# The load of x in column quarters at the head of a two-model transformer kernel

## The reference

```python
h = rms_norm(x, norm_pre[l])        # x * rsqrt(mean(x*x)) * gain
proj = h @ w_in[l]                  # [512, 2048] @ [2048, 5952], then split in 12 parts
... three kinds of attention on the parts, gates, w_out ...
x = x + rms_norm(y, norm_post[l])
```

## Time and profile before

| | |
|---|---|
| median of 3 runs | 3525.47 us (3524.55 to 3526.89) |
| the profiled execution's own time | 3524.82 us |
| its span | 3523.1 us |
| PE busy | 3397.5 us, 96% |
| VectorE busy | 1795.1 us, 51% |
| ScalarE busy | 1099.3 us, 31% |
| DMA over the span | 122 GB/s mean, 429.95 MB |
| mean granted TensorE clock | 0.986 |

### The profile page before, as it was taken

How to read it: one execution, slowest core, us unless ns; L and a number is a source line. 1 busy time by engine, 2 the same in 40 slices (tenths; PEclk the granted TensorE clock), 3 DMA queues, 4 the chain that set the end, 5 groups by cost and what they waited for, 6 DMA issues and landing times. The chain is left out here.

```text
span 3523.1 us, 50023 instructions
## 1 busy us (share of the span) xinstructions
PE 3397.5 (96%) x17285; PEld 2742.2 (78%) x17285; DVE 1795.1 (51%) x3258; ACT 1099.3 (31%) x1768; POOL 152.2 (4%) x218
## 2 busy tenths in 40 slices
PE   7999999999999999999997999999997999999997
PEld 6878878678788788786885888878786888878786
DVE  5564675445565557754456332625734332635643
ACT  3232242242241422522323222523323322423331
POOL 1101001000111010010010000000000000000000
PEclk9999999999999999999998999999998999999999
DMA  7636415215675363160454333133333333123242
GB/s 270 199 118 198 125 37 175 68 69 193 184 243 183 115 188 95 32 205 7 138 180 151 97 95 89 31 99 99 117 124 110 90 95 95 49 87 99 79 155 95
DMA packets 183848, 429.95 MB, mean 122 GB/s; under 512 B 18166, under 2 KB 25777, under 8 KB 177240
## 3 DMA queue, kind: packets, MB, share of 16 engines
q1 hardware_dynamic: 151144, 297.65, 26.3%
q0 software_dynamic: 28992, 104.43, 9.7%
q10 hardware_dynamic: 3504, 25.22, 1.8%
HBM read 406.15 MB, written 24.75 MB: 122 GB/s over the span
## 5 line engine op out<-in xcount | busy, mean ns | idle before, releaser
L681 PE MATMUL bank<-wlo,act_hi 128*128 128x512 f32 (+1 forms) x3968 | 1554.7, 392 | 8.8 <-DVE zone L1597 6.1
L683 PE MATMUL bank<-whi,act_lo 128*128 128x512 f32 (+1 forms) x3968 | 1537.9, 388 | 0.0
L682 PE MATMUL bank<-whi,act_hi 128*128 128x512 f32 (+1 forms) x3968 | 1536.8, 387 | 0.0
L1548 DVE TENSOR_TENSOR wlo<-stage,whi 128x1024 fp32r<-128x1024 f32 (+1 forms) x496 | 598.2, 1210 | 753.8 <-ACT whi L1184 751.5
L1184 ACT ACTIVATE whi<-stage 128x1024 fp32r<-128x1024 f32 (+1 forms) x496 | 514.9, 1048 | 1479.9 <-PE bank L683 734.8
L681 PEld LDWEIGHTS bank<-wlo,act_hi 128*128 128x128 f32 x3968 | 746.7, 188 | 178.2 <-issue 17.8
L683 PEld LDWEIGHTS bank<-whi,act_lo 128*128 128x128 f32 x3968 | 746.3, 188 | 153.3
L682 PEld LDWEIGHTS bank<-whi,act_hi 128*128 128x128 f32 x3968 | 747.1, 188 | 146.8 <-issue 1.0
L1563 DVE SCALAR_TENSOR_TENSOR macc<-wmod,csil,macc 128x512 f32<-128x512 f32 x360 | 269.9, 750 | 106.7 <-DMA wmod<-in_w_mod 76.9
L2415 POOL DMA_DIRECT2D wmod<-in_w_mod x192 | 136.9, 713 | 1706.2 <-DVE macc L1563 1675.0
L744 PE MATMUL bank<-zone 128*128 128x128 f32 x1024 | 134.6, 275 | 0.0
(11 more groups left out here) (239 smaller groups left out, 2269.7 us busy)
## 6 DMA issues: line engine op xcount, KB each, us to landing
stage<-in_w_in SPq DMA_DIRECT2D x352, 512.0 KB, 3.8
wmod<-in_w_mod POOLq DMA_DIRECT2D x192, 512.0 KB, 4.5
stage<-in_w_out SPq DMA_DIRECT2D x128, 512.0 KB, 4.1
out<-Y ACTq DMA_DIRECT2D x20, 1024.0 KB, 5.6
zone<-out SPq DMA_DIRECT2D x4, 4096.0 KB, 14.3
stage<-in_w_in SPq DMA_DIRECT2D x16, 320.0 KB, 3.7
Y<-in_x ACTq DMA_DIRECT2D x4, 1024.0 KB, 9.3
rpb_tiles<-rpb_pad POOLq DMA_DIRECT2D x16, 224.0 KB, 7.6
```

What stands on the lines that cost most here:

```text
L681: pe.matmul(out, hi_x, lo_w, start=(k == 0), stop=False)
L682: pe.matmul(out, hi_x, hi_w, start=False, stop=False)
L683: mm = pe.matmul(out, lo_x, hi_w, start=False, stop=(k == KC - 1))
L1548: dve.tensor_tensor(wlo[:, j % RH, :, 0:width], stage[:, j % RS, :, 0:width], whi[:, j % RH, :, 0:width].bitcast(F32), ALU.subtract).then_ ...
```

## The change

x is loaded in four column quarters (512 features of all 512 tokens, runs of 2 KB) in place of four token tiles (runs of 8 KB), and these loads stand first in ScalarE's queue. PE waits for quarter k // 4 ahead of the turn of tile k, in place of all four parts ahead of the panel. The stores of x go from behind tile 3 to behind tile 15 in ScalarE's order, in both layers. The waits for x and for the residual's second half move to the sums of squares. GpSimd issues panel 0's eight loads of `w_mod` ahead of the bias tiles, in layer 0 only.

```diff
@@ turns (PE)
+                if blk == 0 and n0 == 0 and k % 4 == 0:
+                    pe.wait_ge(boot_x[k // 4], 16)
@@ head of the layer (PE)
-                for t in range(TT):
-                    pe.wait_ge(boot_x[t], 16)
@@ turned_then_saved (ScalarE)
-                    if k == 2 * LEAD - 1:
+                    if k == KC - 1:
                         for t in range(TT):
-                            act.wait_ge(boot_x[t], 16)
                             act.wait_ge(prep.sem, prep.at(0, l, t + 1 - TT))
                             act.dma_start(x_dram[:, t, :], Y[:, t, :]).then_inc(x_saved.sem, 16)
@@ squares_between (ScalarE)
+                    if t == 0:
+                        for q in range(DM // PW):
+                            act.wait_ge(boot_x[q], 16)
                     if 0 <= t < TT:
+                        act.wait_ge(prep.sem, prep.at(0, l, t + 1 - TT))
@@ start of the queue (ScalarE)
+            for q in range(DM // PW):
+                act.dma_start(Y[:, :, q * PW:(q + 1) * PW], x_in[:, :, q * PW:(q + 1) * PW]).then_inc(boot_x[q], 16)
             act.sem_inc(exp_done.sem, exp_done.credit)
...
             act.activation(ctmp[:, :], JOB[0][:, 0:KC], ACT.Tanh, scale=0.5).then_inc(boot_act, 1)
-            for t in range(TT):
-                act.dma_start(Y[:, t, :], x_in[:, t, :]).then_inc(boot_x[t], 16)
@@ GpSimd
+                if l == 0:
+                    mod_loads(l, 0)
                 bias_tiles(l)
-                with pool.Fori(0, NIN) as p:
+                with pool.Fori(1 - l, NIN) as p:
                     mod_loads(l, p)
```

## The result

The change makes the kernel slower: 3532.99 us median (3529.72 to 3536.71, 19 runs) against 3524.75 us (3520.81 to 3527.53, 19 runs) of the kernel before. The ratio is 1.0024, 95% interval 1.0018 to 1.0031, so +8.2 us. The forecast was 3521.9, range 3516.5 to 3527.0. The profiled execution has a span of 3531.3 us, 8.2 above that of before.

The account below looks back on a forecast made before the run. PE, busy 96% of the span, was taken to bound the kernel, so only its idle time counts. The terms -9.0 + 1.4 + 2.0 + 2.0 = -3.6 gave 3521.9 us, range 3516.5 to 3527.

Parts of the forecast that it names:

- The start: Ahead of panel 0's first product: x and weights share DMA in halves, so that product comes 9.0 us earlier.
- the forecast's 14.1: Predicted time of PE's first product, from doubles landing at 10.8, 0.3 to ScalarE's start and a 3.03 us chain.
- doubles that land after 13: At the start: weight doubles 0 and 1 landing later than 13 us would show the prediction wrong.
- quarter 1 "at 12.1": At the start, bound with weights at 60%: doubles land at 9.9, x's quarter 1 at 12.1, first product at 13.
- the gain of 10: At the start, upper bound of the gain in us, with weights taking 60% and the first product at 13.
- The turns: DMA sharing at the start: each engine goes round its queues a packet at a time, giving x and weights halves.
- x's quarters: At the start: quarter 0 lands near 6 and the turns begin; quarter 2, wanted at 27, is in by about 20.
- The clock at the start: First products of panel 0 run at 1.2 GHz after PE idles, costing 1.4 us, bounds 0 and 2.1.
- The ends of panel 0: Moved stores delay pair 7's load and so VectorE's take, costing PE 2.0 us in each layer.
- Bias tiles: Issued behind pair 7's load, they delay panel 1's first w_mod load: cost 0, with 0.8 us to spare.
- The lateness stays small: Rival: delays at both ends of panel 0 cost 0 to 1 us in all, giving 3518.4; chance 0.25.
- The slower rival: Panel 1's first w_mod load lands late behind the bias tiles and stops PE at double 3: 3533; chance 0.06.

Follow-up runs that it names:

- e13: Changed kernel with the stores of x behind tile 15 doubled in bytes, the second copy to an unread tensor: 3539.07 us, ratio 1.0042.
- e10: Changed kernel with stores back behind tile 3 and 54 extra identity turns on PE ahead of the first panel: 3515.66 us, ratio 0.9970.
- e2: Changed kernel with VectorE's take of panel 0 moved ahead of mod pair 7, stores left behind tile 15: 3522.24 us, ratio 0.9996.
- e4: Kernel before with only the loads of x first and in quarters; stores and bias tiles where they were: 3524.51 us, ratio 0.9998.
- e1: Changed kernel with only the four stores of x put back behind tile 3: 3520.9 us, ratio 0.9987.
- e7: Changed kernel with stores back behind tile 3 and 34 extra identity turns on PE ahead of the first panel: 3515.98 us, ratio 0.9977.
- e8: Changed kernel with the stores of x, still behind tile 15, cut into runs of 2 KB in place of 8 KB: 3533.64 us, ratio 1.0025.
- e11: Changed kernel with x quarters 2 and 3 issued behind the weight doubles, one store ahead of each sum of squares, 30 extra identity turns: 3518.03 us, ratio 0.9981.
- e14: Changed kernel with x quarters 2 and 3 issued after double 0 lands, one store ahead of each sum of squares, 38 extra identity turns: 3513.26 us, ratio 0.9970.
- e9: Changed kernel with stores back behind tile 3 and x quarters 2 and 3 issued at 4.23, behind the two weight doubles: 3520.94 us, ratio 0.9987.

## Why the prediction was wrong

It named each place where something happens and gave two of its terms the wrong size; the sign of the sum hung on them. -9.0 + 1.4 + 2.0 + 2.0 became, by the traces, -5.5 + 1.4 + 5.7 + 5.8 = +7.4, against +8.2 measured.

- **The start, -9.0: mis-sized, -5.5.** The failed step is "doubles 0 and 1 and quarter 1 all need 1.05 MB at 0.205 from 5.7, so land at 10.8". The even share was right (515 packets to 465). Wrong were its two ends. The doubles' data began at 7, not 5.7, that is 3.5 us after issue, while x filled the engines. And 0.3 us were given from the last byte to ScalarE's start; the last of the data flowed at about 13, and ScalarE began the cut at 14.32, 1.3 later. Of the 3.6 us by which the first product came later than the forecast's 14.1, 1.3 lie ahead of the data, 0.9 in it, 1.0 behind it, and 0.4 in the chain, whose last turn ran at half speed. Both ends could be read in the kernel before. Its weights, issued at 3.38, moved nothing until 7.5. And the 2.3 us of latency that I had read off x's own first part, which found the engines idle, I put all in front: x, issued at 2.85, moved its first bytes at 3.9, so half of it lies behind the last byte. The prediction's own sign of being wrong here, doubles that land after 13, came true. One bound was also miscounted: quarter 1 "at 12.1" keeps x at 40% after the doubles are through; with the engines to itself it is there at 10.8, and the gain of 10 stays.
- **The turns.** By the Trainium skill (DMA: Bandwidth & Descriptors, Queues, rings and completion order) the engines go round the queues a packet at a time. The runs agree from a queue's first packet on (399 to 392, 407 to 395), though of three queues in e13 the third had only 246. For the 3.5 to 6 us ahead of the first packet, in which the other queue had 99% and more, the rule gives nothing, and the forecast had only 2.3 us there.
- **x's quarters** were early enough, as predicted; the first turn at 8.48 and not near 6, since the rows for its scale came late behind x. It cost nothing: PE waited for the doubles.
- **The clock at the start, +1.4: right**, 4.25 - 2.84 = 1.4. e10 shows the cause, as the gap was taken away and the term went with it. The forecast's reason was the right one: the turns' length told the clock where the window's own figure did not.
- **The ends of panel 0, +2.0 and +2.0: mis-sized, +5.7 and +5.8.** The mechanism, place and releaser were as predicted. Two steps failed. The lateness was sized as two thirds of 2.9 us, by which a load beside the old stores was slower, and of 4.4 in layer 1; it was 3.5 (9.4 against 5.9) and 4.9 (9.3 against 4.4), since the stores did not share: they had everything until 66. And the sum priced PE's wait at its own length. I had put the drop of the clock behind a 2.3 us gap into the start and left it out here: 2.7 us in layer 0, 1.7 in layer 1.
- **Bias tiles, 0: right** in the changed kernel, in part by luck. The first `w_mod` load of panel 1 landed 15.4 us after issue as worked out, and PE waited for no `wlo` in panel 1, but only after the larger loss ahead of it. Where that loss is gone (e2) PE waits 1.03 us here, and 3.74 where the load is slower still (e13). The other half was not seen: moving them is what lets an early start hold (e4 against e1, 3.6 us).
- **The rivals.** "The lateness stays small" had 0.25 and was the farthest from what happened. The slower rival named the right sign at the wrong place; its mechanism is real (e2, e13) but cost nothing in the changed kernel. The right one, both panel ends at full overlap with the clock's price on each, was within reach of the rows: 4 and 3.4 were already the bounds, and with 1.4 to 2.1 of clock on each the sum is -9.0 + 1.4 + 7.4 + 2.8 to 4.2, or 3528 to 3529.5; with 5.5 at the start, 3531.6 to 3533.

Open: why e7 and e10, with extra turns before the first panel, end about 5 us below e1, where their start makes e7 1.3 us later and e10 1.4 earlier. With intervals of 3 us to either side the medians allow a smaller difference; where the rest would come from was not tried. Open too is why a queue's first packet comes late: a fixed time, or bytes that the engines already hold (at 0.41 MB per us, 3.5 to 6 us are some 1.4 to 2.5 MB, an estimate), no run tells apart.

## What to carry to other kernels

A bulk transfer that is moved off one critical path should be followed to whatever is issued on any queue while its data flows: here 4.2 MB of stores, 10 us at 0.41 MB per us, made a 512 KB load of another queue 3.5 to 4.9 us later, and the same stores 1 MB at a time and over before that load cost nothing. A wait of PE is priced with the slow matmuls behind it: 4.12 us of idle came to 6.8 in layer 0, 4.15 to 5.8 in layer 1. And an operation that PE waits for should not stand in one engine's order behind one that waits for a load, if they are independent: `take` ahead of pair 7 removed both gaps though the load was as late as before.

## What the runs showed of the hardware

- While one queue keeps the 16 engines full, another's first packets came 3.5 us (doubles issued at 3.48, first bytes at 7), 4.1 (before, 3.38 to 7.5), about 5 (GpSimd's load issued at 61.12, and at 60.62 in e13) and 6 (e8, 62.09 to 68.1) after the issue. On quiet engines a double of SP's queue began 1.0 us after issue (before, 65.92 to 66.9), and GpSimd's load 2.7 us ('s issued at 65.67, first bytes at 68.4). So the wait was 2.5 to 3.3 us longer. It followed neither the runs' length (2 or 8 KB) nor how much was still queued (2 or 6 MB).
- The granted clock rose and fell with PE's idle time: the products came at 1.2 GHz behind gaps of 3.2 (e7), 4.1, 4.5 (e11) and 4.8 us, but at full speed behind the 2.53 us of e14 and the 0.43 of e10. The earlier trace rows has the lower clock behind 2.3 us of idle, but there the turns ahead of the gap had run at it too. The Trainium skill (TensorE: Matmul & The Clock Gate, What's actually happening) calls the half rate the default that activity lifts; all of these agree.
- The clock of the windows view is not to be trusted in the first 20 us. For e9 it says 1.00 where the matmuls start 0.43 us apart, the pace at 1.2 GHz:

```profile
17.40:20.00 2.60, 2.60 (x9) 2.14 (x8) 2.56 (x4) 0.31 (x1) 0.00 (x0) 1.00 1.05 395
```
